# Three transformer-like blocks in one kernel: five phases rearranged on one core

## The reference, cut to what matters

```
block 1:  h = rmsnorm(x, g_in);  proj = h @ w_in                    # first turn + first projection
          stick-breaking attention, convolution, memory attention, gate, w_out
block 2:  mod = silu([c, c_ctx]) @ w_mod + b_mod                    # made in pieces, some in the filter phase
          filt = sin(freq*(sin(freq*(feats @ w1 + b1)) @ w2 + b2)) @ w3, times a decay
          filt = filt / sum |filt|;  short convolution of three taps   # the filter phase
          hyena, fourier and attention branches, merge
          aff = softmax(h @ w_router)                               # the router, 16 experts
          top_w, top_i = top_k(aff.T, 128);  experts on the picked tokens
block 3:  latent attention -> y_mla;  wkv recurrence over tokens -> y
          y_rw = groupnorm(y) * ln_g + ln_b + bonus
          out = concat(y_mla, y_rw) * silu(z) @ w_out
          h = h + rmsnorm(out, post_g)                              # the last phase
```

## Time and profile before

| what | us |
|---|---|
| median of 3 runs (lowest, highest) | 4691.05 (4685.43, 4695.68) |
| the profiled execution, its own time | 4688.48 |
| its span, first to last instruction | 4686.7 |
| PE busy | 3928.9 (84%) |
| DVE busy | 2748.1 (59%) |
| ACT busy | 1925.6 (41%) |
| POOL busy | 444.7 (9%) |

### The profile page before, as it was taken

One profiled execution on the slowest core, in us unless ns is written; L12 is line 12 of the kernel. 1 busy time (PEld: TensorE's weight loads), 2 busy tenths in 40 slices (PEclk: granted clock), 3 DMA queues, 4 the chain that ended last, 5 costly groups with the idle time before them and its releaser, 6 DMA issues. The chain is left out here.

```text
span 4686.7 us, 51366 instructions
## 1 busy us (share of the span) xinstructions
PE 3928.9 (84%) x18599; PEld 3116.7 (67%) x18599; DVE 2748.1 (59%) x3244; ACT 1925.6 (41%) x2596; POOL 444.7 (9%) x332
## 2 busy tenths in 40 slices
PE   7995775769997886898947999999998898765489
PEld 5884534648882774486836888888886686554477
DVE  4234756341113776475556999999997524546852
ACT  1013534131112664214324777777775302454223
POOL 0000004051000121101000110111010400000010
PEclk8997887889998998899967999999999898887789
DMA  3222233112224003416417999999997232524251
GB/s 99 96 90 79 58 111 84 41 50 98 98 90 170 14 21 126 147 63 205 121 72 291 402 382 390 385 379 382 394 380 291 77 98 92 183 69 139 52 151 60
DMA packets 437535, 765.24 MB, mean 163 GB/s; under 512 B 103143, under 2 KB 265767, under 8 KB 436232
## 3 DMA queue, kind: packets, MB, share of 16 engines
q1 hardware_dynamic: 409272, 691.95, 42.1%
q10 hardware_dynamic: 23504, 54.53, 3.0%
q0 software_dynamic: 4608, 16.78, 1.4%
HBM read 643.77 MB, written 114.82 MB: 162 GB/s over the span
## 5 line engine op out<-in xcount | busy, mean ns | idle before, releaser
L71 PE MATMUL b_in_acc<-b_in_acts_hi,b_in_w_hi 128*128 128x512 f32 (+1 forms) x1456 | 574.8, 395 | 61.0 <-POOL b_in_w_lo L1030 20.9
L72 PE MATMUL b_in_acc<-b_in_acts_lo,b_in_w_hi 128*128 128x512 f32 (+1 forms) x1456 | 571.2, 392 | 0.0
L73 PE MATMUL b_in_acc<-b_in_acts_hi,b_in_w_lo 128*128 128x512 f32 (+1 forms) x1456 | 570.8, 392 | 0.0
L3826 DVE TENSOR_TENSOR experts_w_lo<-top_xT,experts_w_hi 128x2048 fp32r<-128x2048 f32 x192 | 437.3, 2290 | 62.1 <-ACT experts_w_hi L3771 62.1
L3826 DVE TENSOR_TENSOR experts_w_lo<-experts_ring,experts_w_hi 128x2048 fp32r<-128x2048 f32 x192 | 435.8, 2288 | 31.8 <-ACT experts_w_hi L3771 29.6
L66 DVE CAST b_in_w_hi<-b_in_w 128x1024 fp32r<-128x1024 f32 (+1 forms) x91 | 66.7, 734 | 657.5 <-PE b_in_acc L73 642.5
L3771 ACT ACTIVATE experts_w_hi<-top_xT 128x2048 fp32r<-128x2048 f32 x192 | 367.5, 1919 | 127.5 <-PE experts_gate L73 74.5
L3771 ACT ACTIVATE experts_w_hi<-experts_ring 128x2048 fp32r<-128x2048 f32 x192 | 367.6, 1920 | 114.5 <-PE experts_up L73 65.4
L71 PEld LDWEIGHTS b_in_acc<-b_in_acts_hi,b_in_w_hi 128*128 128x128 f32 (+1 forms) x1456 | 275.1, 189 | 128.7 <-POOL b_in_w_lo L1030 21.7
L73 PEld LDWEIGHTS b_in_acc<-b_in_acts_hi,b_in_w_lo 128*128 128x128 f32 (+1 forms) x1456 | 275.3, 189 | 58.9
L72 PEld LDWEIGHTS b_in_acc<-b_in_acts_lo,b_in_w_hi 128*128 128x128 f32 (+1 forms) x1456 | 275.5, 189 | 58.1 <-issue 0.7
(11 more groups left out here) (711 smaller groups left out, 8726.8 us busy)
## 6 DMA issues: line engine op xcount, KB each, us to landing
experts_ring<-in_w_gate SPq DMA_DIRECT2D x128, 1024.0 KB, 7.2
top_xT<-in_w_up SPq DMA_DIRECT2D x128, 1024.0 KB, 9.7
experts_ring<-in_w_down SPq DMA_DIRECT2D x64, 1024.0 KB, 10.0
top_xT<-in_w_down SPq DMA_DIRECT2D x64, 1024.0 KB, 9.5
b_in_w<-in_w_in SPq DMA_DIRECT2D x90, 512.0 KB, 3.9
proj<-b_in_out ACTq DMA_DIRECT2D x90, 512.0 KB, 2.7
x_spill<-top_xT SPq DMA_DIRECT2D x3, 4096.0 KB, 14.4
merge_gate<-proj SPq DMA_DIRECT2D x48, 256.0 KB, 3.9
```

What stands on the lines that cost most here:

```text
L71: nc.tensor.matmul(out, w_hi, x_hi, start=start, stop=False)
L72: nc.tensor.matmul(out, w_hi, x_lo, start=False, stop=False)
L73: return nc.tensor.matmul(out, w_lo, x_hi, start=False, stop=stop)
L3826: nc.vector.tensor_tensor(w_lo[n % HIS][:, :, :], ring[n % RING], w_hi[n % HIS][:, :, :].bitcast(F32), ALU.subtract).then_inc(lo_ready, 1)
```

## The change

1. A phase of its own for the first turn: eight row buffers, all loads issued at once, PSUM in four pairs, VectorE copies one half of the features, ScalarE the other.
2. In the first projection, sums(1) stands ahead of the half tile (0,1,1), when `double` is not set.
3. Filter phase: two accumulators for the modulation rows, copies by ScalarE, the first modulation block alone before the second layer and two after it; the last four table roundings go from before the second sine into the loop; the load order changes.
4. Router: w_router is loaded in the norm phase ahead of its gains. Logits with the router stationary and 512 tokens moving, then turned back. Picks as 32 matmuls with 64 stationary columns and 512 moving ones, four copies, 16 small turns.
5. A buffer `ahead` of 12 x 512 columns is shared: work storage in the first two recurrence phases, then the target of the last phase's first mix, gate and weight loads, issued in the recurrence's last phase after the first four inverses.
6. Last phase: products of part 0 alternate with means and variances; VectorE starts with weights, gating and low parts; eight row buffers; the turn of x is apart from that of the output, and that of items 8 to 15 stands between the last products.

```diff
+def first_turn_phase(nc, name, ident, src_dram, dst):
+    NT, NB, ROWS = T // P, KD // 4, 8
...
+            for s in range(ROWS):
+                sp.dma_start(rows[s][:, :], src_dram[s * P:(s + 1) * P, :]).then_inc(rows_loaded[s], 16)
...
+                for b in range(NB):
+                    if s >= 4:
+                        pe.wait_ge(copied[b], s - 3)
...
+                nc.vector.tensor_copy(dst[:, 0:4, s * P:(s + 1) * P], turned[s % 4][0][:, :, :]).then_inc(copied[0], 1)
...
+                nc.scalar.activation(dst[:, 4:8, s * P:(s + 1) * P], turned[s % 4][1][:, :, :], ACT.Copy).then_inc(copied[1], 1)
...
             sum_squares(0)
+            if not double:
+                sum_squares(1)
             half_tile(0, 1, 1)
-            sum_squares(1)
+            if double:
+                sum_squares(1)
```

Filter phase, SP, TensorE and ScalarE:

```diff
-            for n in range(2):
-                load_mod(n)
+            load_mod(0)
             for j in range(4):
                 load_raw(j)
-            load_mod(2)
+            load_mod(1)
+            sp.dma_start(x_spill[:, :, :], xT[:, :, :]).then_inc(spilled, 16)
             for i in range(2):
                 load_decay(i)
-            sp.dma_start(x_spill[:, :, :], xT[:, :, :]).then_inc(spilled, 16)
-            sp.dma_start(delta[:, :], bias.rearrange("o w -> (o w)").partition_broadcast(P)).then_inc(bias_loaded, 16)
+            load_mod(2)
             load_mod(3)
...
-                if n:
-                    pe.wait_ge(rows_made, n)
-                modulation_rows(nc, made[:, :], mod_w[n % 2], silu, range(KD)).then_inc(mod_used, 1)
+                if n >= 2:
+                    pe.wait_ge(rows_made, n - 1)
+                modulation_rows(nc, made_in(n), mod_w[n % 2], silu, range(KD)).then_inc(mod_used, 1)
...
-                for n in range(2):
-                    modulation(2 * layer + n)
+                for n in range(1 + layer):
+                    modulation(layer + n)
...
-                if i in (1, 2, 3, 4):
+                if i + 3 < 2 * n_steps:
                     modulation(i + 3)
...
             first_tap(1)
-            for j in range(4, NJ):
-                high(j)
+            mod_row(0)
+            mod_row(1)
             sine(1)
...
+                if i + 2 < 2 * n_steps:
+                    mod_row(i + 2)
+                if i + 4 < NJ:
+                    high(i + 4)
```

Router:

```diff
+            for h in range(2):
+                for c in range(KD):
+                    mm = nc.tensor.matmul(aff_ps[h][:, :], w_sb[:, c, :], hT[:, c, h * HALF:(h + 1) * HALF], start=(c == 0), stop=(c == KD - 1))
+                mm.then_inc(logitsT_ready, 1)
             for t in range(NT):
-                for c in range(KD):
-                    mm = nc.tensor.matmul(logits[:, t, :], hT[:, c, t * P:(t + 1) * P], w_sb[:, c, :], start=(c == 0),
-                                          stop=(c == KD - 1))
+                if t % 4 == 0:
+                    pe.wait_ge(logitsT_copied, t // 4 + 1)
+                mm = nc.tensor.matmul(logits[:, t, :], logitsT_sb[:, t * P:(t + 1) * P], ident[0:E, 0:E], start=True, stop=True)
...
-                for e in range(E):
-                    mm = nc.tensor.matmul(picked[:, e, :], sel[t][:, e, :], facts[:, t, e, :], start=(t == 0 and e == 0),
-                                          stop=(t == NT - 1), skip_group_check=True)
+                for g in range(4):
+                    mm = nc.tensor.matmul(cross[g], facts[:, t, :, :].rearrange("p e n -> p (e n)"), sel[t][:, 4 * g:4 * g + 4, :],
+                                          start=(t == 0), stop=(t == NT - 1))
...
+            for e in range(E):
+                if e % 4 == 0:
+                    pe.wait_ge(crossed_copied, e // 4 + 1)
+                mm = nc.tensor.matmul(picked[:, e, :], cross_sb[:, e, :], ident[0:4 * E, 4 * e:4 * e + 4], start=True, stop=True)
```

Recurrence and last phase:

```diff
             for c in range(XT):
                 sp.wait_ge(xt_zeroed, c + 1)
                 load_inverse(c)
+            for dst, rows in ahead_pairs:
+                sp.dma_start(dst, rows).then_inc(ahead_loaded, 16)
...
-            mean(0, 0)
-            for r in range(1, HC):
+            for r in range(HC):
+                products(0, 0, 0, r)
                 mean(0, r)
-                variance(0, r - 1)
+                if r:
+                    variance(0, r - 1)
             variance(0, HC - 1)
...
                             if h == 1 and 1 <= s <= 8:
-                                turn(s - 1)
+                                turn_x(s - 1)
+                                turn_out(s - 1)
+                            if h == 1 and s > 8:
+                                turn_x(s - 1)
             column_sums(2 * NT - 1)
+            turn_x(15)
             for i in range(8, 16):
-                turn(i)
+                turn_out(i)
...
             for n in range(4, NT):
                 evict(NT + n)
+                copy_x(7 + n)
+            copy_x(15)
             inverse_columns(1)
-            for i in range(8, 16):
-                copy_x(i)
```

201 lines of the change are left out of this document (122 added, 79 removed).

## The result

The changed kernel took 4639.76 us (median of 4 runs, 4635.48 to 4648.6) beside 4688.89 for the kernel before on the same chip: ratio 0.9896, interval 0.9877 to 0.9915, 49 us less. The forecast was 4644: a saving of 46.9 us against the median 4691.05 of the kernel before that was known then.

A forecast was written before the change was run, and what follows sets the result against it. Barriers make the time a sum of phases, each bound by its last-ending wait, no engine bounding the whole. Terms -11, -5.7, -18.3, -15.5, +1.9, +1.7 sum to -46.9 against 4691.05: forecast 4644 us, range 4626 to 4664, chance 0.72.

The forecast's parts named there:

- First turn, -11: First turn: eight loads issued at once, phase ends at 21, TensorE at high or low clock; saves 11 us, 7 to 11.5.
- Column sums, -5.7: First projection: sums moved ahead of the last half tile remove TensorE's idle time and low clock; saves 5.7 us, 3.5 to 6.5.
- Filter, -18.3: Filter phase: earlier second sine, no waits for row copies in the loop; saves 18.3 us, 12 to 21.
- the same 5.9 us follow: Filter phase's end: after the last sizes at 124.8, the same 5.9 us as before follow, ending at 130.6.
- Router, -15.5: Router: earlier weight load, long-column logits, and wide picks hidden behind selections; saves 15.5 us, 11 to 18.
- Recurrence, +1.9: Recurrence's last part: ten loads queued ahead delay the inverse of chunk 4, stalling TensorE; costs 1.9 us, 0 to 5.
- 0.67 us for 256 KB ... 8.9 us: Recurrence: queue time of the ten loads, 0.67 us per 256 KB and 1.7 per weight, 8.9 us in all.
- Last phase, +1.7: Last phase: nothing gained before the first eviction, x turns inside products add 2.6, tail changes; costs 1.7 us, 0 to 4.
- Rival 2: Last phase gains through an earlier mean chain, earlier weight rounding and a freer tail: -12 instead of +1.7, total 4630; chance 0.12.
- Rival 1: Router's long-column matmuls stay at low clock, sums take 27 us instead of 16; total 4661 with late filter loads; chance 0.11.
- Rival 3: Recurrence: load queue does not recover, 12 later chunks' inverses are late; at 5 us each total 4704; chance 0.02.
- Rival 4: Change fails its purpose: first-turn loads still go singly and filter taps still wait for the sine; total 4670; chance 0.03.

The follow-up runs named there:

- e6: Changed kernel with two first-turn row buffers, column sums behind the last half tile, one row accumulator, picks with the selection stationary; 4671.66 us, executed once.
- e7: Changed kernel with four table roundings ahead of the second sine, logits with hT stationary, gate_mix(1, r) behind center(1, r); 4658.41 us, executed once.
- e2: Changed kernel with the wait for all eight weight remainders moved from ahead of the first eviction to ahead of the fifth; 4628.40 us.
- e3: Changed kernel with the ten loads for the last phase issued one by one behind the inverse loads of recurrence chunks 2 to 11; 4634.91 us.
- e9: Kernel of e5 with the x turns of items 8 to 15 left behind the last product, as before the change; 4624.04 us, executed once.
- e1: Changed kernel with the recurrence and last-phase lines put back to those of the kernel before; 4630.04 us.
- e5: Kernel of e4 with gating, rounding and low parts of the last phase's first half tile interleaved with its normalisations; 4625.08 us.
- e4: Changed kernel with both the edit of e2 and the edit of e3; 4625.60 us.
- e10: Changed kernel with wait moved, loads spread, chain interleaved, fifth eviction earlier, and the filter's small row turns ahead of its last size matmuls; 4620.83 us.

## Why the prediction was right or wrong

**The total** is right, 4644 against 4639.76 and 4642.71. In part that is luck, because the errors lean against each other: the two losses were 6.5 us larger than forecast and the savings 1.5 smaller, while 5 us came in a phase without an edit. The six touched phases alone give 38.9 us, 8 less than forecast. Two sums of the prediction are off without moving the forecast by more than 0.2: the ends of its terms add up to a saving of 24.5 to 57 us, not 30 to 63, and the router's three parts (2.0, 9.7 and 3.6) to 15.3, not 15.5.

**First turn, -11:** -12.0. The loads landed every 1.25 us, not 1.33; the phase ends at 20.2, forecast 21. Of my two cases for TensorE's clock each held for a part: the view gives 1.00 for the whole stretch, but the first three blocks took 1.7 us each, slower than the loads came, and the next ones 0.87, by which TensorE caught up with the loads ahead of the last. e6 shows that the buffers make 11 of the 12 us.

**Column sums, -5.7:** -5.9, and -6.5 by e6. The products run through from 56.3 on, with no idle time; the mechanism is the forecast one.

**Filter, -18.3:** -17.0. "The second sine at 64.4" is 34.6 us after the start; it is at 34.8. The loads of the modulation weights paced it as I said, e7 gives the sine's place 8.3 us and e6 the second accumulator 6.1. The step that missed is "the same 5.9 us follow": behind the last sizes 8.0 us follow, since the turns that took 4.1 us take 6.98 at the low clock here. That is not a trait of the new code: in e2 the same code turned in 4.24 us and the phase was 20.2 shorter than before. So the term lies between -16.3 and -20.2, by the trace.

**Router, -15.5:** -14.2, with logits 18.7 us to their last small matmul (17.8 forecast). The long matmuls took 16.8 us, 0.8 more than 14.0 and the 2 for the low clock. In the ten traces with this router unchanged the phase took between 99.7 and 104.2 us: the code is the same, the moment at which the clock rises is not (these matmuls took 15.2 to 16.8 us). The picks' last 32 small records scatter with it, from 5.5 to 7.0 us. A saving of 14.2 to 18.7 is all that can be said.

**Recurrence, +1.9:** +5.3. The mechanism is right ("one stall at chunk 4", no later chunk is late), the size is not. The step that failed is the time of the ten loads, "0.67 us for 256 KB ... 8.9 us": the inverse was to land 9.8 us after the first of these issues and landed 14.1 us after it. 2.4 us of the difference are that the first load landed 3.0 us after its issue and not 0.67, 1.7 that the next seven came every 0.91, 0.9 the weights; the inverse itself was 0.5 quicker than I had it. And a second term was missing: the matmuls behind the stall run at the low clock, 1.9 us or more.

**Last phase, +1.7:** +4.9, or +2.6 in e3, where the same code had the fast product group (167.2 us). At the phase's head the contention came as I had put it, the four low parts end 10.7 us after the start, forecast 10.8. "The first eviction still on GpSimd's eighth remainder" holds, but it comes at 52.6 us after the start, not 49.5. norm(0,3) ends at 33.8, forecast 33.0, and the remainders take 2.2 us longer because the second half's gatings, whose inputs now arrive early, run beside them: I had put that contention at the phase's head and not here, and that is the step that failed. The Trainium skill (page "SBUF — State Buffer", section "Who interferes with whom") has the rule that two SBUF inputs on VectorE contend with GpSimd's reads, and the trace agrees here too (5.78 us for a remainder that takes 2.4 alone). The x turns inside the products cost 2.7 by e9, forecast 2.6. The tail is 9.6 us from the last product to the last join, forecast 10.3 (12.9 less the 2.6 of the turns).

**Rival 2** (the last phase gains 12, 0.12) was nearer than the forecast in what is possible: with one wait moved, one chain interleaved and one eviction earlier the phase takes 154.9 us, 9.7 less than before, though not by the causes that the rival named. What kept most of it from showing was a wait that stood for a layout that the change itself had given up. I had read that wait as given. **Rival 1** falls: the long matmuls do rise to the high clock (1.00 in the router's second 7 us). **Rival 3** falls: only one inverse was late (from the phase's first matmul on, PE waits once for an inverse in each trace of the changed kernel, 3.48 and 4.04 us at chunk 4, and in e3 not at all). **Rival 4** falls with the first turn and with e7's sine.

## What to carry to other kernels

When a change moves a buffer, look again at every wait that guarded the old place: here one moved wait gave 10.3 us, a fifth to a quarter of what the whole change had brought. Price a stop of TensorE at more than its length (here 6.0 us for 4.0, the recurrence of the changed kernel's second trace against e1; 8.9 for 5.6), since the matmuls behind it can run slower. Loads for a later phase go between the loads that a running chain waits for, one at a time, and are priced with the rate of loads like them and the time to the first landing. Read a product group or a phase in several traces before giving a microsecond or two of it to an edit: the same code differed by 1.6 us in one group and by 4 us in a phase.

## What the runs showed of the hardware that I had not expected

Behind a stop of only 1.27 us the clock can be low for most of a product group (4.58 us, e5), and behind the same stop it can stay high (3.01 in e4); five traces of eleven show the one and six the other. The clock fell once with no stop at all, behind 3.7 us of two-column matmuls that the profile shows as busy (0.54, e10).

An unbroken row of VectorE instructions can hold up GpSimd for its whole length. VectorE in the changed kernel, the last gatings beside the first remainder (5.78 us, from 4515.18 on):

```profile
4514.41 1.29 DVE L66 CAST last_w_hi<-b3c_ahead 128x1024 fp32r<-128x1024 f32 x2
4515.62 1.29 DVE L66 CAST last_w_hi<-last_out 128x1024 fp32r<-128x1024 f32 x2
4516.82 1.89 DVE L5255 TENSOR_TENSOR b3c_ahead<-b3c_ahead 128x512 f32<-128x512 f32 x3
4519.06 2.45 DVE L5255 TENSOR_TENSOR b3c_ahead<-b3c_ahead 128x512 f32<-128x512 f32 x1 [0.35 <-DMA b3c_ahead<-proj]
```

Casts and three gatings follow each other without a pause and at full pace (0.68 us each) until 4518.71, and the remainder ends at 4520.96, 2.25 us later: about what one takes alone (2.33 to 2.41). In the changed kernel's second trace the distance is 2.25 us again. In the kernel before and in e7 only casts, which have one input in SBUF, stand beside the first remainder; it takes 3.98 us and ends 2.26 us after the last cast. So the remainder seems to have begun its work only when VectorE paused; this is read from the times, no run separates it from a partial slowing. The fourth gating came after a pause of 0.35 us, with GpSimd at work, and it was VectorE's turn to wait: 2.45 us.
